# Projections in plain f32: one matmul per product instead of three on split operands

## What is computed

```python
D_MODEL, SEQ = 1024, 256
FFN_HIDDEN = -(-8 * D_MODEL // (3 * 256)) * 256          # 2816

def swiglu(h, w_up, w_down):
    a, b = jnp.split(h @ w_up, 2, axis=-1)
    return (jax.nn.silu(a) * b) @ w_down

# nsa_attention:      proj = h @ w_in          ...  o @ w_out
# dilated_attention:  q = (h @ w_q)            ...  o @ w_out
# first_block:        kv = (rmsnorm(x, kv_norm) @ kv_w)
# second_block:       h @ w_in[l], merged @ w_out[l], mem @ w_mem_kv[l], swiglu_ffn(...) twice
```

## Time and profile before

| | |
|---|---|
| median of 2 runs | 1306.75 us (1306.72 to 1306.78) |
| the profiled execution | 1304.92 us, span 1303.1 us |
| granted TensorE clock, mean | 0.996 of full speed |
| busy | PE 1270.1, PEld 1059.4, DVE 811.3, ACT 644.9, POOL 271.3 us |
| matmul records, weight load records | 7279, 7279 |
| DMA | 224.77 MB, mean 172 GB/s |

### The profile page before, as it was taken

How to read it: one execution, slowest core, us unless ns; L and a number is a source line. 1 busy time by engine, 2 the same in 40 slices (tenths; PEclk the granted TensorE clock), 3 DMA queues, 4 the chain that set the end, 5 groups by cost and what they waited for, 6 DMA issues and landing times.

```text
span 1303.1 us, 19302 instructions
## 1 busy us (share of the span) xinstructions
PE 1270.1 (97%) x7279; PEld 1059.4 (81%) x7279; DVE 811.3 (62%) x1210; ACT 644.9 (49%) x946; POOL 271.3 (21%) x362
## 2 busy tenths in 40 slices
PE   6999999999999999999999999999999999999997
PEld 5986788888799977888888788888887778888886
DVE  3468675555574486654555755556789877755554
ACT  4438654444453366543444655445444683544442
POOL 6420210000000041102000489701186210200000
PEclk9999999999999999999999999999999999999999
DMA  9970556555455644467655465654544436556651
GB/s 288 273 136 19 166 173 193 182 184 186 159 194 180 177 115 130 161 195 175 228 183 179 167 194 186 220 188 147 194 130 146 146 121 202 181 190 193 191 188 41
DMA packets 155883, 224.77 MB, mean 172 GB/s; under 512 B 13395, under 2 KB 107979, under 8 KB 155820
## 3 DMA queue, kind: packets, MB, share of 16 engines
q1 hardware_dynamic: 141008, 208.36, 50.9%
q0 software_dynamic: 10064, 10.54, 4.3%
q10 hardware_dynamic: 4748, 5.02, 1.1%
HBM read 222.56 MB, written 1.25 MB: 172 GB/s over the span
## 4 chain that ended last, share of the span: by engine, by line
PE 80%; DVE 8%; ACT 4%; DMA 4%; issue 2%; POOL 1%; SPq 0%; DVEq 0%; ACTq 0%; POOLq 0%
PE bank L195 23%; PE bank L197 23%; PE bank L196 23%; PE bank L216 4%; DMA raw_units<-in_a_w_in 3%; DVE units_lo L178 3%; PE bank L204 2%; PE bank L702 1%; DMA raw_units<-in_ffn_w_up 1%; ACT arena L1497 1%; DVE arena L2907 1%; PE bank L211 1%; PE bank L1774 1%; DVE arena L2898 1%; ACT units_hi L170 1%
## 5 line engine op out<-in xcount | busy, mean ns | idle before, releaser
L621 DVE TENSOR_TENSOR units_lo<-raw_units,units_hi 128x2048 fp32r<-128x2048 f32 x96 | 223.1, 2324 | 154.2 <-ACT units_hi L575 154.2
L195 PE MATMUL bank<-units_hi,turned_hi 128*128 128x512 f32 (+1 forms) x792 | 307.0, 388 | 3.1 <-DVE units_lo L178 1.3
L197 PE MATMUL bank<-units_hi,turned_lo 128*128 128x512 f32 (+1 forms) x792 | 302.1, 381 | 0.0
L196 PE MATMUL bank<-units_lo,turned_hi 128*128 128x512 f32 (+1 forms) x792 | 301.7, 381 | 0.0
L178 DVE TENSOR_TENSOR units_lo<-raw_units,units_hi 128x2048 fp32r<-128x2048 f32 (+2 forms) x103 | 232.4, 2265 | 109.3 <-ACT units_hi L170 109.1
L170 ACT ACTIVATE units_hi<-raw_units 128x2048 fp32r<-128x2048 f32 (+2 forms) x103 | 193.2, 1886 | 113.3 <-PE bank L197 83.1
L575 ACT ACTIVATE units_hi<-raw_units 128x2048 fp32r<-128x2048 f32 x96 | 183.5, 1911 | 104.0 <-PE bank L197 95.6
L195 PE MATMUL bank<-units_hi,second_hi 128*128 128x512 f32 (+1 forms) x560 | 219.2, 391 | 0.0
L197 PE MATMUL bank<-units_hi,second_lo 128*128 128x512 f32 (+1 forms) x560 | 216.8, 387 | 0.0
L196 PE MATMUL bank<-units_lo,second_hi 128*128 128x512 f32 (+1 forms) x560 | 216.6, 387 | 0.0
L195 PEld LDWEIGHTS bank<-units_hi,turned_hi 128*128 128x128 f32 x792 | 149.0, 188 | 32.8 <-DVE units_lo L178 3.0
(11 more groups left out here) (352 smaller groups left out, 1789.8 us busy)
## 6 DMA issues: line engine op xcount, KB each, us to landing
raw_units<-in_ffn_w_up SPq DMA_DIRECT2D x88, 512.0 KB, 4.8
raw_units<-in_ffn_w_in SPq DMA_DIRECT2D x88, 512.0 KB, 4.6
raw_units<-in_ffn_w_down SPq DMA_DIRECT2D x22, 1024.0 KB, 4.9
raw_units<-in_ffn_w_out SPq DMA_DIRECT2D x22, 1024.0 KB, 4.9
raw_units<-in_w_in SPq DMA_DIRECT2D x18, 1024.0 KB, 5.0
raw_units<-in_b_w_q SPq DMA_DIRECT2D x12, 1024.0 KB, 5.2
raw_units<-in_a_w_in SPq DMA_DIRECT2D x10, 1024.0 KB, 10.7
raw_units<-in_kv_w SPq DMA_DIRECT2D x6, 1024.0 KB, 5.2
```

The source lines that it names most:

```text
L195: pe.matmul(out, lh, rh, start=start, stop=False, skip_group_check=True)
L196: pe.matmul(out, lh, rl, start=False, stop=False, skip_group_check=True)
L197: return pe.matmul(out, ll, rh, start=False, stop=True, skip_group_check=True)
L621: dve.tensor_tensor(m.WL[:, slot(n0 + j), :], m.RAW[:, slot(n0 + j), :], m.WH[:, slot(n0 + j), :].bitcast(F32), ALU.subtract).then_inc(m.l ...
```

## The change

`mm3` becomes one matmul of what the upper buffers hold, `upper_rows` and `lower_rows` become one function with one matmul (`rows_by_weights`), and the six buffers of rows and weights are declared f32 instead of f32r. ACT's copy into an f32 buffer then holds the whole number, and DVE's subtraction, which stays, writes zeros that no matmul reads. The waits for lower parts stay too. `project_kv_first` runs only its second pass, that with the waits for norm_lo.

```diff
 def mm3(pe, out, lh, ll, rh, rl, start):
 
-    pe.matmul(out, lh, rh, start=start, stop=False, skip_group_check=True)
-    pe.matmul(out, lh, rl, start=False, stop=False, skip_group_check=True)
-    return pe.matmul(out, ll, rh, start=False, stop=True, skip_group_check=True)
-
-
-
-def upper_rows(pe, out, rows_hi, wh, wl, start, stationary=True):
-
-    for x, w in enumerate((wh, wl)):
-        ins = pe.matmul(out, *((rows_hi, w) if stationary else (w, rows_hi)), start=start and x == 0, stop=False,
-                        skip_group_check=True)
-    return ins
-
-
-def lower_rows(pe, out, rows_lo, wh, stationary=True):
-
-    return pe.matmul(out, *((rows_lo, wh) if stationary else (wh, rows_lo)), start=False, stop=True,
-                     skip_group_check=True)
+    return pe.matmul(out, lh, rh, start=start, stop=True, skip_group_check=True)
+
+
+
+def rows_by_weights(pe, out, rows, w, start, stationary=True):
+
+    return pe.matmul(out, *((rows, w) if stationary else (w, rows)), start=start, stop=True, skip_group_check=True)
...
@@ up_half, in ffn_tensor
-                    upper_rows(pe, m.pb[t][:, :], m.HTH[:, k, tok], m.WH[:, sl, col], m.WL[:, sl, col], k == 0)
+                    ins = rows_by_weights(pe, m.pb[t][:, :], m.HTH[:, k, tok], m.WH[:, sl, col], k == 0)
...
                     pe.wait_ge(m.s("tile_lo"), 16 * r + 8 * t + kt + 1)
                 col = slice(k * 512, (k + 1) * 512)
-                if first and half == 0:
-                    ins = lower_rows(pe, m.pb[t][:, :], m.HTL[:, k, tok], m.WH[:, sl, col])
-                else:
+                if not first or half == 1:
                     ins = mm3(pe, m.pb[t][:, :], m.HTH[:, kt, tok], m.HTL[:, kt, tok],
                               m.WH[:, sl, col], m.WL[:, sl, col], kt == 0)
...
@@ project_kv_first
-    for part, ready in enumerate(("norm_hi", "norm_lo")):
+    for part, ready in ((1, "norm_lo"),):
...
@@ mixer_left_upper, mixer_left_lower: the products move into the first, the wait stays in the second
...
-    m.HTH, m.HTL = sb("turned_hi", [P, KT, S], F32R), sb("turned_lo", [P, KT, S], F32R)
-    m.OTH, m.OTL = sb("second_hi", [P, KT, S], F32R), sb("second_lo", [P, KT, S], F32R)
+    m.HTH, m.HTL = sb("turned_hi", [P, KT, S]), sb("turned_lo", [P, KT, S])
+    m.OTH, m.OTL = sb("second_hi", [P, KT, S]), sb("second_lo", [P, KT, S])
     m.RAW = sb("raw_units", [P, 3, ULEN])
-    m.WH, m.WL = sb("units_hi", [P, 3, ULEN], F32R), sb("units_lo", [P, 3, ULEN], F32R)
+    m.WH, m.WL = sb("units_hi", [P, 3, ULEN]), sb("units_lo", [P, 3, ULEN])
```

More of the change, by code:

```diff
@@ L1616, in project_kv_first @@
                 out = m.pb[bank][:, i * S:(i + 1) * S]
[L1617 to L1620, removed]
+                rows_by_weights(pe, out, m.HTH[:, kt, :], m.WH[:, sl, at], kt == 0 and i == 0, False)
             at = slice(k * 512 + S, (k + 1) * 512)
@@ L1623, in project_kv_first @@
                 out, tok = m.pb[bank + 1][:, t * S:(t + 1) * S], slice(t * P, (t + 1) * P)
[L1624 to L1627, removed]
+                ins = rows_by_weights(pe, out, m.HTH[:, kt, tok], m.WH[:, sl, at], kt == 0 and t == 0)
     return ins
@@ L3085, in mixer_left_upper, with mixer_left_lower @@
         k, at = 4 * G + r, slice(r * 512, (r + 1) * 512)
[L3086 to L3096, removed]
+        ins = rows_by_weights(pe, m.pb[DOWN_BANK + 2 * t][:, :], m.OTH[:, k, tok], m.WH[:, slot(n), at], k == 0)
     if t == 1:
         ins.then_inc(m.unit_used, 1)
+def mixer_left_lower(pe, m, G, t):
+    pe.wait_ge(m.s("m_lo"), 2 * G + t + 1)
 def mixer_out_tensor(pe, m):
```

## The result

The changed kernel takes **1570.36 us** (median of 2 runs, 1570.07 to 1570.65) against 1306.75 us before: a ratio of 1.202, 95% interval 1.197 to 1.207. Its profiled execution took 1570.07 us with a span of 1568.3 us.

A forecast was written before the change was run, and what follows sets the result against it. Bound: how fast TensorE starts one matmul after another. 1304.9 + 242.9 + 40.0 + 0.7 - 6 = 1582.5, with the median 1.8 us above: 1584 us, 21% slower; range 1555 to 1630.

The forecast's parts named there:

- Two records per product, two cycles per column: In every product, one plain f32 matmul makes two records: 0.864 us for 512 columns, 0.437 us for 256.
- The count: Products in mm3, upper_rows and four small groups of the view: 1320 with 512 columns, 520 with 256.
- 512 columns: The 1320 products of 512 columns go from 0.680 to 0.864 us each: +242.9 us.
- 256 columns and the later wait: 520 products of 256 columns, 0.360 to 0.437 us: +40.0; project_kv_first waiting for norm_lo instead of norm_hi: +0.7 us.
- Absorbed waits: Some of PE's 33.0 us of idle time shrinks, as slower products give other engines time: -6 us.
- ACT and DVE: ACT's copies and DVE's subtractions, 199 of each, now on f32, stay hidden behind PE: no added time.
- From the execution to the median: The median of the runs lies 1.8 us above the profiled execution, added to 1582.5 us.
- The stages: Feed-forward layer grows from 181 to 230 us, the 256-column stretch of 97 us by 20; attention loops keep their length.
- Loads in the open: Rival: one weight load of 0.113 us per product is exposed, +208 us, 1792 us in all; chance 5%.
- All waits absorbed: Rival: PE's whole 33 us of idle time goes instead of 6, giving 1557 us; chance 5%.
- Two passes: Rival: a product is one half-rate record, 0.432 or 0.2185 us; loading becomes the bound, about 1010 us; chance 3%.
- Does not do what it says: Rival: operands still reach TensorE as f32r, one record each, 1010 us; or time stays at 1305; together 2%.

The follow-up runs named there:

- the earlier wait: The changed kernel with project_kv_first waiting for norm_hi instead of norm_lo: 1565.27 us, and 1565.45 us when repeated beside the changed kernel's 1568.15.

## Why the prediction was right, point by point

**The bound.** PE sets the end in both kernels. The attention loop, a stretch without products, kept its length, and cutting DVE's busy time from 812 to 394 us gave 3 us at most.

**Two records per product, two cycles per column.** Right, and it carries the result. The reading came from six records for three calls and 0.43 us between them. The records fell by 1840, and their steps are 429 and 216 ns.

**The count.** 1320 and 520 products: 2640 and 1040 product records stand in the trace after.

**The sum.** +277.6 us of span was forecast, +265.2 came. The mechanism held, and the miss of 12.4 us is one of sizes. They partly cancel: the 512-column products were forecast 21.1 us too dear, the 256-column ones half a us too cheap, and the rest of the span 8.2 too cheap. By terms:
- *512 columns, +242.9 forecast, +221.8 measured.* This term was mis-sized in three places. The 5 ns on top of a record are 2.5: 2640 x (0.432 - 0.4292) = -7.4 us. The three records before cost 0.2314 us each on the mean and not the 0.2267 of one undisturbed place, since the waits and late weight loads at the heads of units and stages are in the mean: 3960 x 0.0047 = -18.6. The mean after is 0.4311 and not 0.4292: +5.0.
- *256 columns and the later wait, +40.7 forecast, +41.2 measured.* The sum is nearly right by luck, since its parts are not those forecast. The record is 3 ns shorter (-2.8 us), and the records before took 0.1221 us on the mean and not 0.120 (-3.3). Against that, the records after took 0.2228 on the mean for an undisturbed 0.2158 (+7.3): 2.5 of it stand in `project_kv_first` and 1.7 in products at 95 us, both at the low clock that the kernel before does not have there (0.94 on the mean from 75 to 98 us, where it was 1.00). The prediction priced the wait at 0.7 us for its idle time alone, and did not reckon with the clock.
- *Absorbed waits, -6 forecast.* Taken as idle time this was right: it fell from 33.0 to 1568.3 - 1540.7 = 27.6 us. But the prediction took idle time for all that could be absorbed. At the head of a unit the first product's second record often comes late, and no idle time shows, since the modelled end of the first record covers the gap:

```profile
213.37 0.48 PE L195 MATMUL bank<-units_hi,turned_hi 128*128 128x512 f32 x1
213.69 0.39 PE L196 MATMUL bank<-units_lo,turned_hi 128*128 128x512 f32 x1
213.92 0.40 PE L197 MATMUL bank<-units_hi,turned_lo 128*128 128x512 f32 x1
```

From 213.37 to 213.69 are 0.32 us, where 0.227 is usual. The second record's weight load began at 213.46 only, behind that of the first, where in the undisturbed stream it begins with the record before. The trace before has 101 steps of 0.06 to 0.2 us more than usual, 80 of them from a product's first record to its second, 9.7 us together, and the one after 37, 3.6 us. They, a part of the idle time and some 500 steps that were a few ns longer than usual make up the 18.6 - 5.0 = 13.6 us that went within the first term. This is the step that was read too low. Outside the products the span grew by 2.2 us, and 1.7 of them are gone again in the trace with the earlier wait.
- *ACT and DVE:* nothing, as forecast.
- *From the execution to the median:* 1.8 us were carried over, 0.3 were measured.

**The stages.** 230 us were forecast for a feed-forward stretch of 181, +49; the measured growth is 46.0. For keys and queries 20 were forecast and 21.7 measured.

**The rivals.** *Loads in the open* did not come: a step of 0.429 has no room for 0.113. A late load shows at the heads of streams: 0.50 to 0.53 us for such a step, where 0.429 is usual. *All waits absorbed* did not come either. *Two passes* did not come; had it been so, the price would have been wrong by some 30 to 60 us, since the other engines hold a product of 0.453 us at 1068 us, and the loads do not hold it at 1010. *Does not do what it says* is excluded by the types and counts above.

## What to carry over

Where TensorE is the bound, count records times step, for the type at hand, from a place in the trace where such records follow one another; and take the step of the work that is removed as the mean over all its records, not from its cleanest place. Fewer instructions in the source are not fewer passes: one plain f32 matmul is four passes over the columns, three f32r matmuls are three, and here a product went from 0.680 to 0.858 us, a quarter more, and the kernel became a fifth slower. A cheaper product has to be priced by the stage, since the next bound (here the other engines in the mixer and ahead of it, DVE busy for 185 of 214 us) is reached in one stage long before another.

## What was not expected of the hardware

- A record of f32r on the full array steps by its columns at 2.4 GHz and 13 ns more (0.227 and 0.120 us); one of plain f32, at two cycles per column, by 2 to 3 ns more (0.429 and 0.216). Four f32r records are 50 ns slower than one plain f32 product. It is the same in the kernel with one f32r matmul per product, where undisturbed records step by 0.227 too, so it does not come from three matmuls per product. What it comes from was not tried. The Trainium skill, page "TensorE: Matmul & The Clock Gate", section "Back-to-back issue gap", gives N / 2.4 + 2.5 ns for a single matmul of N columns at full clock, and about 131 ns per matmul of 512 columns in a sustained stream. Taken for each record with two cycles per column, the trace agrees for plain f32 (429 and 216 ns); for f32r it does not (227 and 120 where the formula has 216 and 109), and there the measurement decides. The 131 ns show in no run: no 512-column record of f32r steps by less than 224.
- With one f32r matmul per product the granted clock was 0.84 on the mean: PE worked in bursts (690 of 1021 us busy) and the clock fell to 1.2 GHz again and again. Whether that costs time, where PE is busy for two thirds only, was not tried.
